# Score blocks of gated linear attention on 32-wide column tiles, in one stretch, and the head norm's sum as two rounded parts

## The chip, the cores and the metric

The kernel runs on one core of a Trainium2 chip. The metric is the time on the device in microseconds (us): the median of three runs, 2439.63 us, between 2439.05 and 2439.84. The engines are TensorE (PE in the rows; PEld is its loading of weights), VectorE (DVE), ScalarE (ACT), GpSimd (POOL) and SyncE (SP). Each runs its own instructions in order and waits for others on semaphores.

## The reference, cut to what matters

The model has two layers, an even one (retention and a gated linear recurrence) and an odd one (gated linear attention, GLA), each followed by an MLP. It handles 1024 prompt positions and 8 samples of 8 positions, so 1088 columns in all. The change lies in the odd layer. For each of 4 heads:

```python
def step(s, blk):                      # one chunk of the sequence
    qc, kc, vc, gc = blk
    b = jnp.cumsum(gc, axis=1)
    diff = b[:, :, None] - b[:, None, :]
    w = jnp.exp(jnp.where(causal, diff, -jnp.inf))
    scores = jnp.einsum('bihd,bjhd,bijhd->bhij', qc, kc, w)
    o = einsum(scores, vc) + einsum(qc * jnp.exp(b), s)
    s = s * jnp.exp(b_last)[..., None] + einsum(kc * jnp.exp(b_last - b), vc)
    return s, o
...
o = head_rms(o) * norm_w               # head_rms: x * rsqrt(mean(x*x) + EPS)
mix = (silu(r) * o) @ w_out
```

The weight `w` depends on row, column and channel at once, so the scores are not one plain product of q and k.

## The kernel before, in words

Activations lie with channels on the 128 partitions and positions along the columns. The 1088 columns are handled in groups of 384, 384 and 320. Each large projection multiplies two rounded parts: the high part of a weight tile (WH) by the high and the low part of the activation (RA or RB), and the low part of the weight (WL) by the high part; these are the many matmuls of L732, recorded in pairs WH, WH and single WL. In the records a tile of the rounded type is called f32 too.

In the odd layer a chunk is 128 positions (8 for each head, and a ninth of 64 sample positions). The order of all work there is one list, `odd_schedule` (L232), which every engine walks. For a chunk (h, c) it has these items:

- `S`: a group of a projection, cut in two halves of 12 matmuls of L732. They fill the time of TensorE between the items of the chunk.
- `A`: three transposes (L1211, L1213) of decayed keys and values, then the full 128x128 product of keys and queries (L1220), then the coarse levels of the score (L1153).
- `A2`: the fine levels (L1159). Between `A` and `A2` lies one half of an `S`.
- `B`: the output product and the update of the state, of the chunk one place earlier.
- `CO`, `CU`: the same for the samples of the ninth chunk, with very narrow matmuls.

The scores come from seven levels. At level v the chunk is cut in blocks of 2 x 2^v positions; the right half's queries meet the left half's keys, both scaled relative to the middle of the block (tile `gLV`, inside GA). The coarse levels v = 6, 5, 4 write their rectangle straight into the square of the score bank; the fine levels v = 3 to 0 each make a whole 128 x 64 product beside it, of which VectorE then copies only the blocks near the diagonal with a predicate (L2495, L2499). The levels are made by VectorE (L2450 differences, L2475 to L2479 products) with ScalarE's exponentials (L1750 to L1754) between; TensorE waits for each level with `lev_ready`. `gsc_done` tells VectorE that a chunk's scores are there, `gsc_masked` that a score bank is free again. Ordinary fp32 matmuls (all those on GA, SMALL and ONES) are recorded as two passes, each with its own weight load.

The head norm: `GN1` squares the two halves of a head's output (ScalarE, L1791) and adds them (VectorE, L2541); `GNM` multiplies the sum by a matrix of ones to add over partitions (L1300) and ScalarE takes its logarithm (L1798); `GN2` scales the output. This happens 11 times with a `GNM` of its own; the twelfth is L1307.

Of the kernel before, what the change touches and what calls it, by code (L numbers as in the profile page):

```python
# [35 lines left out]
SPLIT = 4  # L36
# [265 lines left out]
def build(nc, xT, ws, prm_in, csa, csg, cs_in, wla, wli, wg2_in, st_ret, st_lru, st_conv, st_gla,  # L302
          yT, retp_o, rets_o, lru_o, conv_o, glap_o, glas_o, x_spill):
    ctx = ExitStack()
    with ctx:  # L305
# [26 lines left out]
        ONES = sb("ONES", [P, P])  # L332
# [160 lines left out]
        gSQ = OD[:, 1792:2560]  # L493
        gSC = [MK[:, 0:CH], MK[:, CH:2 * CH]]
# [43 lines left out]
        def place(h, c):  # L538

            return PLACES.index((h, c))  # L540

# [188 lines left out]
        def _(pe):  # L730
# [61 lines left out]
            def rms_group(g, r):  # L792

                s, size = GROUPS[g]
                nc.tensor.matmul(PS[:, ms_bank(r, g), 0:size], ONES[:, :], RS[:, s:s + size],
                                 start=True, stop=True).then_inc(ms_done, 1)
# [158 lines left out]
            def last_rms(g):  # L955

                s, size = ENDS[g]
                pe.wait_ge(square_used, 7 * 4 + 7 * (g + 1) - g // 2)
                if g:
                    pe.wait_ge(rs_log, 3 * 4 + g)  # L960
                if g < 2:
                    nc.tensor.matmul(PS[:, 7, 0:size], ONES[:, :], RS[:, s:s + size],
                                     start=True, stop=True).then_inc(ms_done, 1)
                else:

                    nc.tensor.matmul(PS[:, 7, 0:size], ONES[:, :], RS[:, s:s + size], start=True, stop=False,
                                     skip_group_check=True)
                    pe.wait_ge(square_ready, 8 * 4 + KT * 3)
                    nc.tensor.matmul(PS[:, 7, 0:size], ONES[:, :], last_square(KT - 1, size), start=False, stop=True,
                                     skip_group_check=True).then_inc(ms_done, 1)  # L970


            def head_sum(item):

                g, h = item[1:]
                size = GROUPS[g][1]
                if h == 0:
                    pe.wait_ge(rn_sq, g + 1)

                    pe.wait_ge(kv_copied, 2 * before("RA", item))  # L980
                if h == 2:
                    pe.wait_ge(sc_masked, before("RA", item))
                if h == 3 and g < 2:
                    pe.wait_ge(s_updated, states_before(item))
                nc.tensor.matmul(PS[:, norm_bank(g, h), 0:size], ONES[:, :], NB[:, h, 0:size],
                                 start=True, stop=True).then_inc(rn_ms, 1)

            ident = CST[:, A_ID:A_ID + P]
            for item in even:
                kind = item[0]  # L990
                if kind in "GS":
                    u = item[1]
                    if u == 0:

                        pe.wait_ge(consts_set, 1)
                        for _ in range(16):
                            nc.tensor.matmul(PS[:, 7, 0:P], ONES[:, :], ONES[:, :], start=True, stop=True)
# [139 lines left out]
            def score(h, c, levels):  # L1137
# [5 lines left out]
                last = None  # L1143
                for v in reversed(levels):

                    pe.wait_ge(lev_ready, nth("Q", e, v))
                    both = gLV[e % 2][:, v, loc:loc + n]
                    if v >= FINE:

                        width = 1 << v  # L1150
                        for left in range(0, n, 2 * width):
                            right = slice(left + width, left + 2 * width)
                            last = nc.tensor.matmul(flat[left:left + width, right], both[:, left:left + width], both[:, right],  # L1153
                                                    start=True, stop=True)
                        continue
                    keys = both if v else gK(h)[:, s:s + n]
                    at = n + n // 2 * v
                    out = flat[0:n, at:at + n // 2].rearrange("p (b n) -> p b n", n=1 << v)
                    last = nc.tensor.matmul(out, keys, halves(both, v)[1], start=True, stop=True)  # L1159
                return last  # L1160

            ident = CST[:, G_ID:G_ID + P]
            for item in odd:
# [30 lines left out]
                elif kind == "A":  # L1194
# [21 lines left out]
                    if k > 1:  # L1216

                        pe.wait_ge(gsc_masked, k - 1)
                    flat = PS[:, score_bank(k), :]
                    nc.tensor.matmul(flat[0:n, 0:n], gK(h)[:, s:s + n], gQ(h)[:, s:s + n], start=True, stop=True)  # L1220
                    score(h, c, range(SPLIT, LEVELS) if c < LAST else ())
                elif kind == "A2":
                    h, c = item[1:]
                    score(h, c, range(SPLIT) if c < LAST else range(SLEVELS)).then_inc(gsc_done, 1)
# [68 lines left out]
                elif kind == "GNM":  # L1293
                    h, g = item[1:]
                    size = GROUPS[g][1]
                    if (h, g) != (GH - 1, 2):
# [3 lines left out]
                        nc.tensor.matmul(PS[:, 7, 0:size], ONES[:, :], gSQ[:, 0:size], start=True, stop=True).then_inc(gn_ms, 1)  # L1300

            def last_head_sum():
# [3 lines left out]
                for v in range(2):  # L1306
                    last = nc.tensor.matmul(PS[:, 7, 0:320], ONES[:, :], gSQ[:, 384 * v:384 * v + 320], start=v == 0, stop=v == 1)  # L1307
# [13 lines left out]
        def _(act):  # L1321
# [34 lines left out]
            def rstd(r):  # L1356
                other(ACT.Ln)
                act.wait_ge(consts_set, 2)
# [341 lines left out]
            for item in odd:  # L1700
# [36 lines left out]
                elif kind == "XE":  # L1737
# [6 lines left out]
                    if v == 0:  # L1744
                        s = GROUPS[g][0]
                        act.wait_ge(b_ready, softened(e))
                        if e > 1:

                            act.wait_ge(gsc_done, 3 * (e - 1))
# [59 lines left out]
                elif kind in ("MIX", "MH"):  # L1809
                    k = item[1]  # L1810
                    if k == 0:

                        act.wait_ge(gsc_done, len(PLACES))
# [31 lines left out]
        def _(dve):  # L1845
# [522 lines left out]
            for item in odd:  # L2368
# [34 lines left out]
                elif kind == "SPD":  # L2403
# [4 lines left out]
                    for c in range(3 * g0, 3 * g1):  # L2408
                        s, n = CHUNKS[c]
                        keep = ONES[:, 0:n] if c < LAST else CST[:, G_RS:G_RS + TS]  # L2410
# [29 lines left out]
                elif kind == "X":  # L2440
# [4 lines left out]
                    if e > 1:  # L2445

                        dve.wait_ge(gsc_done, 3 * (e - 1))
# [34 lines left out]
                elif kind == "A2":  # L2482
# [6 lines left out]
                    dve.wait_ge(gsc_done, k + 1)  # L2489
# [45 lines left out]
                elif kind == "GN1":  # L2535
# [5 lines left out]
                    V.tensor_tensor(gSQ[:, 0:size], gSQ[:, 0:size], gSQ[:, 384:384 + size], ALU.add).then_inc(gn_sum, 1)  # L2541
# [189 lines left out]
```

## Time and profile before

| | before |
|---|---|
| median of 3 runs | 2439.63 us |
| profiled execution, its own time | 2441.21 us |
| its span | 2439.1 us |
| PE busy | 2423.2 us (99%) |
| PE weight loads busy | 2380.3 us (98%) |
| DVE busy | 1305.2 us (54%) |
| POOL busy | 1211.9 us (50%) |
| ACT busy | 796.2 us (33%) |
| mean granted TensorE clock | 0.993 |

Busy is the time in which at least one instruction of the engine was under way. Matmuls are pipelined, so the duration of one (its latency) says little; what one costs is the distance from its start to the start of the next. The chunks of the odd layer lie between 1202 and 1592 us of the span. The granted clock is 1.00 at 2.4 GHz and 0.50 at 1.2 GHz; a mean between them says how much of a stretch ran at either.

### The profile page before, as it was taken

How to read it: one execution, taken by the hardware profiler on the slowest of the kernel's cores; microseconds unless marked ns; L12 is line 12 of the kernel's file. 1: busy time of each engine (PE TensorE's matmuls, PEld its weight loads, DVE VectorE, ACT ScalarE, POOL GpSimd, SP SyncE). 2: the span in 40 equal slices, each digit the busy share in tenths (PEclk: the TensorE clock that was granted, in tenths of full speed). 3: DMA queues.
4: the chain of work that ended last, by engine and by line, in shares of the span. 5: the costliest groups of instructions: out<-in, count | busy, mean ns of one | idle time of the engine just before them, and what ended most of it. 6: DMA issues, size and time to landing. Idle time of an engine off the chain costs nothing. (4 is left out here: it accounts for less than half of the span.)

```text
span 2439.1 us, 42031 instructions
## 1 busy us (share of the span) xinstructions
PE 2423.2 (99%) x16160; PEld 2380.3 (98%) x16160; DVE 1305.2 (54%) x2047; ACT 796.2 (33%) x1254; POOL 1211.9 (50%) x1445
## 2 busy tenths in 40 slices
PE   9999999999999999999999999999999999999998
PEld 9999999999999999999999999999999999999998
DVE  6763354345545545566666665554345545445566
ACT  4711442222222223223444564442222222222234
POOL 2454136465675666675201111146565665666681
PEclk9999999999999999999999999999999999999999
DMA  4123031111111111113111111131111111111112
GB/s 151 35 63 89 26 119 44 53 44 44 52 44 44 52 53 41 47 53 117 47 42 63 47 50 58 34 128 44 44 44 53 53 44 44 53 45 43 53 53 83
DMA packets 41023, 140.04 MB, mean 57 GB/s; under 512 B 6320, under 2 KB 10032, under 8 KB 39696
## 3 DMA queue, kind: packets, MB, share of 16 engines
q1 hardware_dynamic: 32768, 106.78, 13.8%
q10 hardware_dynamic: 8080, 30.78, 3.5%
q8 instruction: 128, 2.10, 0.4%
q14 instruction: 47, 0.39, 0.0%
HBM read 120.42 MB, written 14.88 MB: 55 GB/s over the span
## 5 line engine op out<-in xcount | busy, mean ns | idle before, releaser
L732 PE MATMUL PS<-RB,WH 128*128 128x384 f32 (+1 forms) x4368 | 1087.7, 330 | 0.0
L732 PEld LDWEIGHTS PS<-RB,WH 128*128 128x128 f32 x4368 | 773.5, 189 | 7.5 <-issue 3.6
L732 PE MATMUL PS<-RA,WH 128*128 128x272 f32 (+2 forms) x3520 | 769.0, 309 | 1.3 <-DVE RA L1868 0.7
L732 PE MATMUL PS<-RB,WL 128*128 128x384 f32 (+1 forms) x2232 | 731.6, 328 | 0.0
L638 POOL TENSOR_TENSOR WH<-WR,FEW 128x256 fp32r<-128x256 f32 x420 | 320.1, 792 | 622.3 <-PE PS L732 593.0
L732 PEld LDWEIGHTS PS<-RA,WH 128*128 128x128 f32 x3520 | 586.9, 188 | 5.8 <-DVE RA L1868 1.0
L732 PE MATMUL PS<-RA,WL 128*128 128x272 f32 (+2 forms) x1760 | 540.6, 307 | 0.0
L732 PEld LDWEIGHTS PS<-RB,WL 128*128 128x128 f32 x2232 | 421.4, 189 | 0.0
L642 POOL TENSOR_TENSOR WL<-WR,WH 128x256 fp32r<-128x256 f32 x420 | 372.8, 917 | 0.0
L732 PEld LDWEIGHTS PS<-RA,WL 128*128 128x128 f32 x1760 | 330.7, 188 | 0.0
L1967 DVE TENSOR_TENSOR X<-PS,X 128x544 f32<-128x544 f32 x280 | 202.6, 724 | 205.2 <-PE PS L732 205.1
L1908 DVE SCALAR_TENSOR_TENSOR RAW<-PS,RS 128x384 f32<-128x384 f32 (+1 forms) x192 | 97.0, 533 | 351.1 <-PE PS L732 317.9
L732 PE MATMUL PS<-RA,WS 128*128 128x272 f32 x2016 | 272.1, 288 | 0.0
L732 PEld LDWEIGHTS PS<-RA,WS 128*128 128x128 f32 x2016 | 260.5, 188 | 0.0
L661 POOL TENSOR_TENSOR WL<-WR,WH 128x512 fp32r<-128x512 f32 x168 | 155.2, 938 | 183.4 <-ACT WH L1400 183.4
L650 POOL TENSOR_TENSOR WL<-WR,WH 128x256 fp32r<-128x256 f32 x88 | 67.0, 792 | 336.5 <-ACT WH L1698 336.5
L1381 ACT ACTIVATE RAW<-RAW 128x384 f32<-128x384 f32 (+1 forms) x192 | 92.2, 505 | 332.2 <-DVE RAW L1908 332.2
L1919 DVE TENSOR_TENSOR RA<-RAW,RA 128x544 fp32r<-128x544 f32 (+1 forms) x112 | 142.9, 1294 | 26.3 <-ACT RA L1389 17.4
L661 POOL TENSOR_TENSOR WS<-WR,WS 128x256 fp32r<-128x256 f32 x112 | 119.1, 1064 | 14.6 <-ACT WS L1413 14.6
L1967 DVE TENSOR_TENSOR GA<-PS,GA 128x544 f32<-128x544 f32 x112 | 81.2, 725 | 80.0 <-PE PS L732 79.3
L1892 DVE TENSOR_TENSOR X<-PS,EB 128x384 f32<-128x384 f32 (+1 forms) x48 | 25.4, 535 | 116.6 <-PE PS L732 116.6
L1348 ACT ACTIVATE RB<-X,FEW 128x1088 fp32r<-128x1088 f32 x24 | 28.7, 1205 | 161.9 <-DVE X L1892 125.7
(237 smaller groups left out, 2370.8 us busy)
## 6 DMA issues: line engine op xcount, KB each, us to landing
WR<-ws SPq DMA_DIRECT2D x189, 512.0 KB, 3.5
EB<-xT ACTq DMA_DIRECT2D x8, 544.0 KB, 5.9
x_spill<-X ACTq DMA_DIRECT2D x8, 544.0 KB, 3.1
EB<-x_spill ACTq DMA_DIRECT2D x8, 544.0 KB, 6.8
GA<-st_gla ACTq DMA_DIRECT2D x4, 1024.0 KB, 4.8
glas_o<-GA ACTq DMA_DIRECT2D x4, 1024.0 KB, 4.6
yT<-X SPq DMA_DIRECT2D x16, 208.0 KB, 1.9
X<-xT ACTq DMA_DIRECT2D x4, 544.0 KB, 6.0
```

Of the source, the lines that this page charges most:

```text
L638: nc.gpsimd.tensor_tensor(WH[:, slot, QC * q:QC * (q + 1)], WR[:, slot, QC * q:QC * (q + 1)], ZERO[:, 0:1].to_broadcast([P, QC]), ALU.add) ...
L642: nc.gpsimd.tensor_tensor(WL[:, slot, QC * q:QC * (q + 1)], WR[:, slot, QC * q:QC * (q + 1)], WH[:, slot, QC * q:QC * (q + 1)].bitcast(F32 ...
L650: nc.gpsimd.tensor_tensor(WL[:, slot, QC * q:QC * (q + 1)], WR[:, slot, QC * q:QC * (q + 1)], WH[:, slot, QC * q:QC * (q + 1)].bitcast(F32 ...
L661: return nc.gpsimd.tensor_tensor(out, of, high.bitcast(F32), ALU.subtract)
L732: return nc.tensor.matmul(out, lhsT, rhs, start=start, stop=stop, skip_group_check=True)
L1348: A(dst[:, 0, k, :], X[:, k, :], ACT.Copy, scale=scale).then_inc(h_high, counts)
L1381: A(RAW[:, j, grp(g)], RAW[:, j, grp(g)], ACT.Square).then_inc(sq_done, 1)
L1892: V.tensor_tensor(X[:, m, s:s + size], PS[:, bank(n0 + m, g), 0:size], EB[:, at(m), s:s + size], ALU.add).then_inc(psum_free, 2)
L1908: V.scalar_tensor_tensor(RAW[:, j, s:s + size], PS[:, 3 * (j % 2) + g, 0:size], 0.0, RS[:, s:s + size], ALU.max, ALU.mult).then_inc(psum_f ...
L1919: return V.tensor_tensor(BS[:, slots, 1, q, :], of, BS[:, slots, 0, q, :].bitcast(F32), ALU.subtract)
L1967: last = V.tensor_tensor(pair_of(to), PS[:, bank0:bank0 + 2, 0:BN], pair_of(to), ALU.add)
```

## The change

1. The scores of a chunk are all computed in item `A2`, behind the half `S`; item `A` keeps only the transposes. The wait for a free score bank (`gsc_masked`) moves with them.
2. Each score matmul is cut in blocks of 32 rows of output (`BLOCK`), each of which uses 32 columns of weights. The 128x128 product of keys and queries becomes four products 32x32 on the diagonal; level 6 becomes two of 32x64; levels 5 and 4 stay as they are, on tiles of 32 and 16; each fine level becomes four products of 32x16.
3. `gsc_done` is raised by the matmul of level 0 of each block, so four times per chunk, and the waits on it count blocks (`scored`).
4. For the head norm VectorE now makes, after the sum, a rounded high part and the rest as a rounded low part (two more instructions), and `GNM` becomes two matmuls of the rounded type in place of one of fp32. For that the matrix ONES is of the rounded type, and made by a tensor_scalar at the start; other users read it as fp32 (`ONE`).

```diff
-        ONES = sb("ONES", [P, P])
+        ONES = sb("ONES", [P, P], F32R)
+        ONE = ONES[:, :].bitcast(F32)
...
+        gSQR = RAWR[:, :, :].rearrange("p k t -> p (k t)")[:, 1792:2560]
...
+        def scored(places):
+            return sum(CHUNKS[c][1] // BLOCK for _, c in PLACES[:places])
...
-            def score(h, c, levels):
+            def score(h, c):
...
-                for v in reversed(levels):
+                key, query = gK(h)[:, s:s + n], gQ(h)[:, s:s + n]
+                block = lambda b: slice(b, b + BLOCK)
+                for b in range(0, n, BLOCK):
+                    nc.tensor.matmul(flat[block(b), block(b)], key[:, block(b)], query[:, block(b)], start=True, stop=True)
+                for v in reversed(range(LEVELS if c < LAST else SLEVELS)):
                     pe.wait_ge(lev_ready, nth("Q", e, v))
                     both = gLV[e % 2][:, v, loc:loc + n]
+                    width = 1 << v
                     if v >= FINE:
-                        width = 1 << v
                         for left in range(0, n, 2 * width):
                             right = slice(left + width, left + 2 * width)
-                            last = nc.tensor.matmul(flat[left:left + width, right], both[:, left:left + width], both[:, right],
-                                                    start=True, stop=True)
+                            for b in range(left, left + width, BLOCK):
+                                rows = slice(b, b + min(width, BLOCK))
+                                nc.tensor.matmul(flat[rows, right], both[:, rows], both[:, right], start=True, stop=True)
                         continue
-                    keys = both if v else gK(h)[:, s:s + n]
                     at = n + n // 2 * v
-                    out = flat[0:n, at:at + n // 2].rearrange("p (b n) -> p b n", n=1 << v)
-                    last = nc.tensor.matmul(out, keys, halves(both, v)[1], start=True, stop=True)
-                return last
+                    for b in range(0, n, BLOCK):
+                        out = flat[block(b), at + b // 2:at + (b + BLOCK) // 2].rearrange("p (b n) -> p b n", n=width)
+                        last = nc.tensor.matmul(out, (both if v else key)[:, block(b)], halves(both[:, block(b)], v)[1],
+                                                start=True, stop=True)
+                        if v == 0:
+                            last.then_inc(gsc_done, 1)
...
-                    if k > 1:
-                        pe.wait_ge(gsc_masked, k - 1)
-                    flat = PS[:, score_bank(k), :]
-                    nc.tensor.matmul(flat[0:n, 0:n], gK(h)[:, s:s + n], gQ(h)[:, s:s + n], start=True, stop=True)
-                    score(h, c, range(SPLIT, LEVELS) if c < LAST else ())
                 elif kind == "A2":
                     h, c = item[1:]
-                    score(h, c, range(SPLIT) if c < LAST else range(SLEVELS)).then_inc(gsc_done, 1)
+                    if place(h, c) > 1:
+                        pe.wait_ge(gsc_masked, place(h, c) - 1)
+                    score(h, c)
...
-                        nc.tensor.matmul(PS[:, 7, 0:size], ONES[:, :], gSQ[:, 0:size], start=True, stop=True).then_inc(gn_ms, 1)
+                        mm(PS[:, 7, 0:size], ONES[:, :], gSQR[:, 384:384 + size], True, False)
+                        mm(PS[:, 7, 0:size], ONES[:, :], gSQR[:, 0:size], False, True).then_inc(gn_ms, 1)
...
-            V.memset(ONES[:, :], 1.0).then_inc(consts_set, 1)
+            link(V.memset(EPST[:, 1:2], 1.0))
+            V.tensor_scalar(ONES[:, :], EPST[:, 1:2].to_broadcast([P, P]), 0.0, None, ALU.add).then_inc(consts_set, 2)
             V.memset(EPST[:, 0:1], EPS).then_inc(consts_set, 1)
-            V.memset(EPST[:, 1:2], 1.0).then_inc(consts_set, 1)
...
-                    V.tensor_tensor(gSQ[:, 0:size], gSQ[:, 0:size], gSQ[:, 384:384 + size], ALU.add).then_inc(gn_sum, 1)
+                    first, second = gSQ[:, 0:size], gSQ[:, 384:384 + size]
+                    link(V.tensor_tensor(first, first, second, ALU.add))
+                    link(V.tensor_scalar(gSQR[:, 384:384 + size], first, 0.0, None, ALU.add))
+                    V.tensor_tensor(gSQR[:, 0:size], first, gSQR[:, 384:384 + size].bitcast(F32), ALU.subtract).then_inc(gn_sum, 1)
```

TensorE's rows of one full chunk, from the transposes to a few matmuls behind the fine levels, as they stand before (L732 on RB and WH or WL is the projection, GA holds keys, queries and levels; the sizes are those of the output):

```order
L1213 MATMUL PS<-CST,GA 128x128 x2
L1220 MATMUL PS<-GA 128x128
L1153 MATMUL PS<-GA 64x64
L1153 MATMUL PS<-GA 32x32 x2
L1153 MATMUL PS<-GA 16x16 x4
L732 MATMUL PS<-RB,WH 128x384 x2
...
L732 MATMUL PS<-RB,WL 128x384
L1159 MATMUL PS<-GA 128x64 x4
L732 MATMUL PS<-RB,WH 128x384 x2
```

And the same place of TensorE's program as it stands now (L738 is the old L732, L1226 the old L1213):

```order
L1226 MATMUL PS<-CST,GA 128x128 x2
L738 MATMUL PS<-RB,WH 128x384 x2
...
L738 MATMUL PS<-RB,WL 128x384
L1152 MATMUL PS<-GA 32x32 x4
L1164 MATMUL PS<-GA 32x64 x2
L1164 MATMUL PS<-GA 32x32 x2
L1164 MATMUL PS<-GA 16x16 x4
L1169 MATMUL PS<-GA 32x16 x16
L738 MATMUL PS<-RB,WH 128x384 x2
```

Twelve score matmuls in two places have become 28 in one, behind the half projection.

VectorE's rows around the first `GN1`, before (L2522 updates the state, L2450 makes level differences, L2541 adds the squares, L2495 begins the predicated copies of a chunk's scores):

```order
L2522 SCALAR_TENSOR_TENSOR SMALL<-SMALL,PS 128x256
L2450 TENSOR_TENSOR GA<-X 128x256
L2541 TENSOR_TENSOR SMALL<-SMALL 128x384
L2495 COPY_PREDICATED SMALL<-CST,PS 128x128
L2499 COPY_PREDICATED SMALL<-CST,PS 128x64
```

And now, with the old L2450 as L2461, L2541 as L2553 and L2495 as L2506:

```order
L2461 TENSOR_TENSOR GA<-X 128x256
L2553 TENSOR_TENSOR SMALL<-SMALL 128x384
L2554 TENSOR_SCALAR RAWR<-SMALL 128x384
L2555 TENSOR_TENSOR RAWR<-SMALL,RAWR 128x384
L2506 COPY_PREDICATED SMALL<-CST,PS 128x128
```

Two instructions stand between the sum and the next chunk's copies, 11 times in the program.

## Rows read from the trace of the kernel before

**Rows 1.** The page: the span, then each engine's busy time and share.

```profile
span 2439.1 us, 42031 instructions
PE 2423.2 (99%) x16160; PEld 2380.3 (98%) x16160; DVE 1305.2 (54%) x2047; ACT 796.2 (33%) x1254; POOL 1211.9 (50%) x1445
```

**Rows 2.** Windows of the odd layer's chunks: length, busy us of each engine, granted clock.

```profile
1255.00:1271.00 16.00, 16.00 (x93) 14.62 (x92) 6.73 (x18) 6.18 (x14) 2.77 (x4) 0.79 0.09 34
1350.00:1366.00 16.00, 16.00 (x104) 15.00 (x106) 10.04 (x23) 11.29 (x24) 3.12 (x4) 0.89 0.11 34
1450.00:1470.00 20.00, 20.00 (x119) 18.62 (x118) 10.68 (x25) 11.74 (x23) 3.13 (x4) 0.84 0.09 27
1580.00:1590.00 10.00, 10.00 (x69) 9.06 (x69) 3.16 (x8) 2.75 (x5) 2.56 (x4) 0.83 0.01 2
1200.00:1600.00 400.00, 398.37 (x2895) 377.47 (x2894) 245.59 (x659) 198.69 (x405) 65.56 (x88) 0.97 0.15 50
```

**Rows 3.** Timeline of TensorE, item A of a chunk: start us, length of the group.

```profile
1215.29 0.27 PE L1211 MATMUL PS<-CST,GA 128*128 128x128 f32 x1
1215.39 0.38 PE L1213 MATMUL PS<-CST,GA 128*128 128x128 f32 x2
1215.61 0.39 PE L1220 MATMUL PS<-GA 128*128 128x128 f32 x2
1215.93 0.55 PE L1153 MATMUL PS<-GA 128*64 128x64 f32 x14
1216.41 0.62 PE L732 MATMUL PS<-RB,WH 128*128 128x384 f32 x2
1216.87 0.35 PE L732 MATMUL PS<-RB,WL 128*128 128x384 f32 x1
1217.05 0.52 PE L732 MATMUL PS<-RB,WH 128*128 128x384 f32 x2
```

**Rows 4.** Timeline of TensorE, item A2 of the chunk before that one.

```profile
1211.43 1.00 PE L1159 MATMUL PS<-GA 128*128 128x64 f32 x8
1212.24 0.59 PE L732 MATMUL PS<-RB,WH 128*128 128x384 f32 x2
1212.67 0.33 PE L732 MATMUL PS<-RB,WL 128*128 128x384 f32 x1
1212.85 0.51 PE L732 MATMUL PS<-RB,WH 128*128 128x384 f32 x2
```

**Rows 5.** Window on L1153 alone: length, PE busy and matmuls under way, PEld busy.

```profile
1216.18:1216.30 0.12, 0.12 (x12) 0.11 (x12) 1.00 0.00 0
```

**Rows 6.** Timeline of TensorE around two GNM, of 384 and of 320 columns.

```profile
1237.52 0.81 PE L1300 MATMUL PS<-SMALL,ONES 128*128 128x384 f32 x2
1238.16 0.27 PE L1211 MATMUL PS<-CST,GA 128*128 128x128 f32 x1
...
1302.44 0.70 PE L1300 MATMUL PS<-SMALL,ONES 128*128 128x320 f32 x2
1302.98 0.27 PE L1211 MATMUL PS<-CST,GA 128*128 128x128 f32 x1
```

**Rows 7.** Timeline of VectorE at the first GN1.

```profile
1233.45 0.56 DVE L2541 TENSOR_TENSOR SMALL<-SMALL 128x384 f32<-128x384 f32 x1 [1.32 <-ACT SMALL L1791]
```

**Rows 8.** Line L1159: what its engine's idle time waited for (us, times).

```profile
  DVE GA L2479: 3.7, 7
  DVE GA L2475: 0.5, 2
```

**Rows 9.** Timelines of VectorE and TensorE around one such wait.

```profile
1506.46 0.56 DVE L1884 TENSOR_TENSOR SMALL<-PS,RS 128x384 f32<-128x384 f32 x1 [3.77 <-PE PS L732]
1521.21 0.88 DVE L2475 TENSOR_TENSOR GA<-GA 128x192 f32<-128x192 f32 x1
1522.14 0.43 PE L1159 MATMUL PS<-GA 128*128 128x64 f32 x2 [0.16 <-DVE GA L2475]
```

**Rows 10.** Timeline of TensorE at the start of the program.

```profile
1.07 6.15 PE L997 MATMUL PS<-ONES 128*128 128x128 f32 x32 [1.07 <-DVE FEW L2094]
7.66 0.59 PE L732 MATMUL PS<-RA,WH 128*128 128x384 f32 x2 [0.45 <-DVE RA L2107]
```

**Rows 11.** Timeline of TensorE in the first head's ninth chunk.

```profile
1256.91 4.05 PE L732 MATMUL PS<-SMALL,GA 128*128 128x8 f32 x24
```

More of the change, by code:

```diff
@@ L794, in rms_group @@
                 s, size = GROUPS[g]
-                nc.tensor.matmul(PS[:, ms_bank(r, g), 0:size], ONES[:, :], RS[:, s:s + size],
+                nc.tensor.matmul(PS[:, ms_bank(r, g), 0:size], ONE, RS[:, s:s + size],
                                  start=True, stop=True).then_inc(ms_done, 1)
@@ L961, in last_rms @@
                 if g < 2:
-                    nc.tensor.matmul(PS[:, 7, 0:size], ONES[:, :], RS[:, s:s + size],
+                    nc.tensor.matmul(PS[:, 7, 0:size], ONE, RS[:, s:s + size],
                                      start=True, stop=True).then_inc(ms_done, 1)
                 else:
-                    nc.tensor.matmul(PS[:, 7, 0:size], ONES[:, :], RS[:, s:s + size], start=True, stop=False,
+                    nc.tensor.matmul(PS[:, 7, 0:size], ONE, RS[:, s:s + size], start=True, stop=False,
                                      skip_group_check=True)
                     pe.wait_ge(square_ready, 8 * 4 + KT * 3)
-                    nc.tensor.matmul(PS[:, 7, 0:size], ONES[:, :], last_square(KT - 1, size), start=False, stop=True,
+                    nc.tensor.matmul(PS[:, 7, 0:size], ONE, last_square(KT - 1, size), start=False, stop=True,
                                      skip_group_check=True).then_inc(ms_done, 1)
@@ L984, in head_sum @@
                     pe.wait_ge(s_updated, states_before(item))
-                nc.tensor.matmul(PS[:, norm_bank(g, h), 0:size], ONES[:, :], NB[:, h, 0:size],
+                nc.tensor.matmul(PS[:, norm_bank(g, h), 0:size], ONE, NB[:, h, 0:size],
                                  start=True, stop=True).then_inc(rn_ms, 1)
@@ L996, in _ @@
                         for _ in range(16):
-                            nc.tensor.matmul(PS[:, 7, 0:P], ONES[:, :], ONES[:, :], start=True, stop=True)
+                            nc.tensor.matmul(PS[:, 7, 0:P], ONE, ONE, start=True, stop=True)
                         first_step(0, RA0, 0)
@@ L1306, in last_head_sum @@
                 for v in range(2):
-                    last = nc.tensor.matmul(PS[:, 7, 0:320], ONES[:, :], gSQ[:, 384 * v:384 * v + 320], start=v == 0, stop=v == 1)
+                    last = nc.tensor.matmul(PS[:, 7, 0:320], ONE, gSQ[:, 384 * v:384 * v + 320], start=v == 0, stop=v == 1)
                 last.then_inc(gn_ms, 1)
@@ L2409, in _ @@
                         s, n = CHUNKS[c]
-                        keep = ONES[:, 0:n] if c < LAST else CST[:, G_RS:G_RS + TS]
+                        keep = ONE[:, 0:n] if c < LAST else CST[:, G_RS:G_RS + TS]
                         if c == LAST:
```

13 lines of the change are left out of this document (6 added, 7 removed).

## The prediction

> **What bounds the kernel now.** I read the page first: TensorE is busy 2423.2 of 2439.1 us, VectorE 54%, ScalarE 33% [rows 1]. So the time is the sum of TensorE's distances from start to start, and an edit counts by what it does to that sum, unless it makes TensorE wait. The windows of the odd layer say the same for the 400 us in which the change lies: 398.37 us busy for TensorE, 245.59 for VectorE, 198.69 for ScalarE [rows 2]. Next I read the timelines of one chunk, which give starts. The reader should ignore the lengths there (0.27 us for one transpose is its latency; the next starts 0.11 later).
>
> **The scores, part by part.** There are 32 full chunks (4 heads of 8). In one of them, before:
> - KQ and the coarse levels run from 1215.61 to 1216.41, 0.80 us [rows 3]. The first three projection matmuls behind them take 1216.41 to 1217.05, 0.64, where three such matmuls otherwise take 0.52 (173 ns each: 1217.05 is followed by the same pattern all along, and in rows 4 the WL at 1212.67 starts 0.18 before the next). That is 0.12 lost at the change of kind.
> - The fine levels: 1211.43 to 1212.24, 0.81, and 0.61 in place of 0.52 behind them, 0.09 lost [rows 4].
> Together 1.82 us per chunk.
>
> After the change I count, in passes (two per fp32 matmul): 4 diagonal products 8, level 6 4, level 5 4, level 4 8, fine levels 32, so 56 passes in one block. I call T the time from the first of their starts to where the last is through with its tile. Around T stand: the transposes now run into the projection, 0.09, as L1159 did [rows 4]; going from 128-wide weights to narrow ones, 0.10 (the two KQ passes and the coarse block start 0.32 apart, where two passes of 128 cost 0.11 each, as the transposes do: 0.32 - 0.22) [rows 3]; coming back, 0.11, and 0.12 on the first projection matmuls as now [rows 3]. After = 0.42 + T, and the saving per chunk is 1.40 - T.
>
> What is T? The trace of before has no such block, so I bound it from both sides.
> - Low end: the tiles work side by side. In the window 1216.18 to 1216.30 twelve passes of 32 and 16 columns are under way within 0.12 us, 10 ns each [rows 5]; one pass of 32x32 alone cannot be that short, since a pass with 128 columns of weights costs 0.81/8 = 0.10 us [rows 4], so one of 32 about 0.025. Four column tiles each take a quarter of the passes; the fullest has 2 diagonal, 2 of level 6 (64 moving columns, double), 2 of level 5, 2 of level 4 and 8 fine ones, 16 passes or 18 counts of 0.028: T = 0.50, and 0.90 us saved per chunk, 29 us in all.
> - High end: 14 passes of L1153 take 1215.93 to 1216.41, 34 ns each [rows 3]. With 56 of them T = 1.90 and every chunk costs 0.50 more, +16 us.
> Between ends so far apart I go by the row that it is nearest to. The 34 ns hold two changes of tile width inside them, which the new block does not have, so the 10 ns of rows 5 are nearer; but those twelve passes are a short run that may have been waiting ready in TensorE's queue, while 56 passes and 56 weight loads have to be issued. I take 18 ns, T = 1.0, 0.40 saved per chunk: 32 x 0.40 = 12.8 us.
>
> Here the Trainium skill speaks against the change. "TensorE: Matmul & The Clock Gate", section "Back-to-back issue gap", gives small matmuls a floor of about 25 ns from start to start. By that figure the estimate would be 56 x 25 ns = 1.40 us, and the saving would be nil. The trace does not agree for a short run: twelve passes in 0.12 us [rows 5] are 10 ns each. No row of before shows a long one.
>
> The fourth kind, the ninth chunk of each head (4 in all, 16 passes in place of 8, the same two changes of width): I cost it at nothing, within 0.3 us each.
>
> **Waits in front of the scores.** The levels come from VectorE, and TensorE already waits for them: 3.7 us over 7 and 0.5 over 2 occasions, its weight loads and matmuls counted apart [rows 8]. One of them in detail: VectorE gets its input from TensorE at 1506.46, and from there its own chain with ScalarE runs 15.6 us to the end of level 0 at 1522.09, upon which TensorE starts at 1522.14 [rows 9]. What TensorE saves between those two moments it gives back as waiting. A group of three chunks lasts 400/12 = 33 us, so half of its saving (15.6 of 33) is lost where the levels are that late. Taking half of the 12 groups for it: 12.8 x 1/2 x 1/2 = 3.2 us lost. Queued behind the waiting matmul is all of TensorE's program, so such a wait counts in full. Moving KQ and the coarse levels behind the half projection softens this only by what little of them now stands before the late level; I give it nothing.
>
> The wait for a free score bank moves to a later place; it was not a wait before, and stays none.
>
> **The norm.** A GNM of fp32 costs 1238.16 - 1237.52 = 0.64 us at 384 columns and 0.54 at 320 [rows 6]. Two rounded matmuls cost 2 x 0.173 = 0.35 and 2 x 0.147 = 0.29. So 8 x 0.29 + 3 x 0.25 = 3.1 us less. VectorE does two instructions more, each about the 0.56 us of the sum [rows 7], 11 times, 12 us of an engine with over 150 us free in this stage [rows 2]. They end at about 1235.1 in place of 1234.0, and the GNM starts at 1237.52 [rows 6, 7]: hidden, by the projection half in between. Behind them on VectorE stands the copy of the next chunk's scores, which is needed only a chunk (about 10 us) later. If that cover were gone, it would cost up to 1.1 us x 11 = 12 us.
>
> **The start.** ONES is ready some 0.2 us later. TensorE's warm-up with it is followed by a wait of 0.45 us for VectorE's first operand [rows 10]: hidden.
>
> **The sum.** -12.8 + 3.2 - 3.1 = -12.7 us. The profiled execution's own time is 2441.21 us, 2.1 above its span, and the median shown is 2439.63, 1.6 below it; the saving carries over whole: 2439.6 - 12.7 = 2426.9, say 2427. What a measurement of this kernel can tell from no change is 0.2%, 4.9 us.
>
> **The rivals.**
> - *Full overlap.* The tiles bind and not the issue: T = 0.50. -29 us, of which the late levels keep more (a quarter, 7), and -3 for the norm: 2415. For it speak the twelve passes of rows 5; against it that nothing shows so dense a stream for longer. 0.13.
> - *The pace of issue eats it.* If the passes come no faster than one in 24 to 26 ns, T is 1.34 to 1.46 and the scores give 2 to -2 us; only the norm's 3 remain: 2435 to 2439. This is what the skill's floor in the same section would do (2436.5 by its 25 ns). Against it: rows 5. 0.15.
> - *The slower side: the narrow stream costs as in the block of now.* One mechanism, in the 32 blocks of A2: TensorE can't issue or load the narrow passes at under 34 ns, because each brings its own weight load and the wait on a level at its head. +16 - 3 = +13: 2453. It decides from a pace of about 26.7 ns on, where the scores lose what the norm gains. For it: the only long block in the trace has that pace [rows 3]. Against it: its inner changes of width. 0.10.
> - *VectorE's chain takes it.* If the levels are late in nearly all groups once TensorE is faster, half of everything is lost, and the two new instructions of GN1 push the chain a further 1.1 us in some: -12.8/2 - 3.1 + 4 = -5.5: 2434. For it: 9 waits are there already [rows 8]. Against: VectorE is idle 150 us of 400, much of it waiting for TensorE [rows 2, 9]. 0.10.
> - *The clock.* Around each head's ninth chunk the clock falls to 1.2 GHz (means 0.79, 0.89, 0.84, 0.83 over 16, 16, 20, 10 us: 3.4 + 1.8 + 3.2 + 1.7 = 10 us lost) [rows 2], from the matmuls with 8 moving columns on [rows 11]. If the narrow blocks make it fall once more per group, at the 1.7 us of the smallest of these, 12 x 1.7 = 20 us are lost: 2447. Against: the coarse block of 16 and 32 columns ran at 1.00 [rows 5]. One fall more or fewer at a head's end moves any case by 1.7. 0.06.
>
> My forecast has 0.46, with a range of its own of 2419 to 2435 (T from 0.78 to 1.22).
>
> **How the numbers follow.** Faster by more than 4.9 us: the forecast, full overlap, and most of the chain's case, 0.46 + 0.13 + 0.09, and a little of the pace's case, 0.03: 0.71. Same: 0.12 + 0.01 + 0.01 and a little: 0.14. Slower: 0.10 + 0.05: 0.15. The range reaches from 2413, beyond full overlap, to 2446: it leaves out the 34 ns case and the worst of the clock, and little below.
>
> **What would show each step.** In the timeline after, one block on GA between two projection matmuls; T is the distance from the first start on L1152 to the start of L738 behind L1169 less 0.11: 1.0 if I am right, 0.5 or 1.9 for the rivals. The sum over PE's score lines would fall. L1169's idle time on VectorE's products should grow from some 2 us of matmuls to about 5; the GNM's two matmuls should stand 0.35 us in all, with no wait for L2555. The windows of rows 2 should show the clock at 0.97 over the stage. I am wrong if T is over 1.2, if the waits for levels exceed 6 us, or if the granted clock falls in windows without narrow sample work.

## The result and the profile after

The changed kernel takes 2410.49 us in the median of 4 runs (2410.07 to 2411.48), the kernel before beside it 2439.34: a ratio of 0.9882, with a 95% interval of 0.9870 to 0.9894. That is 28.9 us less. The forecast was 2427 with a range from 2413 to 2446, so the direction was right, the size was not, and the time lies outside the range. The profiled execution of the kernel before took 2441.21 us, 1.9 above the median beside the changed kernel, that of the changed kernel 2410.41, at its median: the two profiles differ by more than the medians do.

The page of the changed kernel, to be read against [rows 1]: TensorE still bounds it, with 33 us less busy.

```profile
span 2408.5 us, 44166 instructions
PE 2390.0 (99%) x17216; PEld 2348.4 (98%) x17216; DVE 1317.0 (55%) x2069; ACT 796.1 (33%) x1254; POOL 1221.6 (51%) x1445
```

TensorE's timeline of one chunk, the same place as [rows 3] and [rows 4] (start us, length of the group):

```profile
1207.95 0.27 PE L1224 MATMUL PS<-CST,GA 128*128 128x128 f32 x1
1208.06 0.38 PE L1226 MATMUL PS<-CST,GA 128*128 128x128 f32 x2
1208.20 0.60 PE L738 MATMUL PS<-RB,WH 128*128 128x384 f32 x2
1208.63 0.35 PE L738 MATMUL PS<-RB,WL 128*128 128x384 f32 x1
1208.82 0.52 PE L738 MATMUL PS<-RB,WH 128*128 128x384 f32 x2
...
1210.22 0.34 PE L738 MATMUL PS<-RB,WL 128*128 128x384 f32 x1
1210.48 0.27 PE L1152 MATMUL PS<-GA 128*32 128x32 f32 x8
1210.57 0.35 PE L1164 MATMUL PS<-GA 128*32 128x64 f32 x15
1210.75 0.21 PE L1169 MATMUL PS<-GA 128*32 128x16 f32 x3
1210.77 0.18 PE L1164 MATMUL PS<-GA 128*16 128x16 f32 x1
1210.80 0.45 PE L1169 MATMUL PS<-GA 128*32 128x16 f32 x29
1211.18 0.62 PE L738 MATMUL PS<-RB,WH 128*128 128x384 f32 x2
1211.63 0.34 PE L738 MATMUL PS<-RB,WL 128*128 128x384 f32 x1
1211.81 0.51 PE L738 MATMUL PS<-RB,WH 128*128 128x384 f32 x2
```

All 56 passes of a chunk start between 1210.48 and 1211.18, where the projection goes on: 0.70 us in place of 0.80 + 0.81, and T, without the 0.11 of the return, is 0.59. Note also that passes of L1169 start at 1210.75, ahead of one of L1164 at 1210.77, though it stands before them in the program: column tiles work each for itself.

The norm's first sum, as in [rows 6]:

```profile
1235.14 0.34 PE L738 MATMUL PS<-RB,WL 128*128 128x384 f32 x1
1235.56 0.59 PE L738 MATMUL PS<-RAWR,ONES 128*128 128x384 f32 x2
1235.99 0.27 PE L1224 MATMUL PS<-CST,GA 128*128 128x128 f32 x1
```

This one takes 0.43 us from start to start; 7 of the 8 of 384 columns take 0.35 to 0.36 in place of 0.64, and the 3 of 320 take 0.30 in place of 0.54. VectorE's side of it, as in [rows 7]:

```profile
1232.07 0.56 DVE L2553 TENSOR_TENSOR SMALL<-SMALL 128x384 f32<-128x384 f32 x1 [1.32 <-ACT SMALL L1802]
1232.67 0.36 DVE L2554 TENSOR_SCALAR RAWR<-SMALL 128x384 fp32r<-128x384 f32 x1
1233.06 0.56 DVE L2555 TENSOR_TENSOR RAWR<-SMALL,RAWR 128x384 fp32r<-128x384 f32 x1
1233.54 0.30 DVE L2506 COPY_PREDICATED SMALL<-CST,PS 128x128 f32<-128x128 uint32 x1
...
1234.94 0.47 DVE L2533 SCALAR_TENSOR_TENSOR SMALL<-SMALL,PS 128x256 f32<-128x256 f32 x1
```

The two parts are ready at 1233.6, 1.9 us before the sum. But the sum also waits for the update of the state (L2533), which stands behind them on VectorE and ends at 1235.4. It starts 0.42 us behind the projection's last matmul; the other ten start 0.15 to 0.18 behind theirs, and so does the first one in the run with the scores alone, where VectorE's two instructions are missing and the update ends at 1234.2. The two instructions thus cost about 0.25 us here, and nothing that shows at the other ten places.

TensorE's waits in the odd layer (us in total, times, longest), and two blocks in which they fall, in the timeline:

```profile
PE PS L1169 <- DVE GA L2490: 3.4, 8, 0.8
```

```profile
1223.46 0.24 PE L1169 MATMUL PS<-GA 128*32 128x16 f32 x6
1224.37 0.26 PE L1169 MATMUL PS<-GA 128*32 128x16 f32 x8 [0.67 <-DVE GA L2490]
1224.91 0.53 PE L1169 MATMUL PS<-GA 128*32 128x16 f32 x16 [0.28 <-DVE GA L2490]
...
1423.81 0.26 PE L1152 MATMUL PS<-GA 128*32 128x32 f32 x4
1424.87 0.24 PE L1169 MATMUL PS<-GA 128*32 128x16 f32 x4 [0.81 <-DVE GA L2490]
1425.35 0.47 PE L1169 MATMUL PS<-GA 128*32 128x16 f32 x8 [0.23 <-DVE GA L2490]
```

TensorE waits in front of level 2 and again in front of level 1. I measured each of the 36 blocks from its first start to the start behind it. Without a wait a full one lasts 0.70 and one of a ninth chunk 0.36; what goes beyond adds up to 6.5 us (0.35 of it, at 1251, is a wait for ScalarE behind the block). The same count before (0.81 and 0.46 for item A2) gives 3.2 us.

The stretches of the stage in which the clock stood at 1.2 GHz: the sum over five windows of before, then over four of after.

```profile
1466.84:1470.25 3.41, 3.41 (x12) 3.41 (x12) 0.76 (x2) 0.00 (x0) 0.00 (x0) 0.50 0.00 0
...
sum 20.46, PE 20.46 PEld 18.32 DVE 8.51 ACT 5.45 POOL 6.84; mean PE 4.09 PEld 3.66 DVE 1.70 ACT 1.09 POOL 1.37
```

```profile
1437.01:1443.83 6.82, 6.82 (x25) 6.09 (x22) 6.72 (x14) 4.89 (x10) 3.75 (x4) 0.50 0.00 0
...
sum 17.03, PE 17.03 PEld 15.65 DVE 12.77 ACT 6.91 POOL 5.81; mean PE 4.26 PEld 3.91 DVE 3.19 ACT 1.73 POOL 1.45
```

Half of that time is lost: 10.2 us before, 8.5 after. This holds for these two executions, not for the kernels. Other executions of the kernel before took from 2434.28 us, at a mean granted clock of 0.996, to 2441.33, at 0.994, so the same program loses some us more or less to the clock; the profiled one is among the slower. The account of the two profiled spans:

| | us |
|---|---|
| 32 blocks, 1.61 to 0.70 | -29.1 |
| 4 blocks of a ninth chunk, 0.26 + 0.46 to 0.36 | -1.4 |
| changes of kind around them, 0.21 before; 0.09 in, 0.11 out and 0.01 behind the transposes after | 0 |
| longer waits for levels, 3.2 to 6.5 | +3.3 |
| the norm's sums, 8 x 0.29 + 3 x 0.24 | -3.0 |
| 3.4 us less at 1.2 GHz | -1.7 |
| new waits of the projection (L738) for VectorE, outside the blocks | +0.6 |
| sum | -31.3 |
| difference of the spans, 2408.5 - 2439.1 | -30.6 |

The other 0.7 us I have not traced.

### The profile page after: what moved, and what is told of

It is laid out like the page before. It is cut to its first block and busy times, and to the rows that moved or that the text cites. A ratio compares the mean times of both kernels' runs of the same rounds, so it can differ in the third digit from the quotient of the medians.

```text
span 2408.5 us, 44166 instructions
## 1 busy us (share of the span) xinstructions
PE 2390.0 (99%) x17216; PEld 2348.4 (98%) x17216; DVE 1317.0 (55%) x2069; ACT 796.1 (33%) x1254; POOL 1221.6 (51%) x1445
## 5 line engine op out<-in xcount | busy, mean ns | idle before, releaser
L738 PE MATMUL PS<-RB,WH 128*128 128x384 f32 (+1 forms) x4368 | 1086.7, 330 | 0.0
L738 PEld LDWEIGHTS PS<-RB,WH 128*128 128x128 f32 x4368 | 773.2, 189 | 6.4 <-issue 3.3
L738 PE MATMUL PS<-RA,WH 128*128 128x272 f32 (+2 forms) x3520 | 769.1, 309 | 1.6 <-DVE RA L1879 0.7
L738 PE MATMUL PS<-RB,WL 128*128 128x384 f32 (+1 forms) x2232 | 731.4, 328 | 0.0
L738 PEld LDWEIGHTS PS<-RA,WH 128*128 128x128 f32 x3520 | 586.9, 188 | 6.1 <-DVE RA L1879 1.0
L738 PE MATMUL PS<-RA,WL 128*128 128x272 f32 (+2 forms) x1760 | 540.6, 307 | 0.0
L738 PEld LDWEIGHTS PS<-RB,WL 128*128 128x128 f32 x2232 | 421.3, 189 | 0.0
L738 PEld LDWEIGHTS PS<-RA,WL 128*128 128x128 f32 x1760 | 330.7, 188 | 0.0
L738 PE MATMUL PS<-RA,WS 128*128 128x272 f32 x2016 | 272.1, 288 | 0.0
L738 PEld LDWEIGHTS PS<-RA,WS 128*128 128x128 f32 x2016 | 260.5, 188 | 0.0
L1359 ACT ACTIVATE RB<-X,FEW 128x1088 fp32r<-128x1088 f32 x24 | 28.7, 1206 | 160.7 <-DVE X L1903 125.3
```

Source lines behind the costliest of these rows:

```text
L738: return nc.tensor.matmul(out, lhsT, rhs, start=start, stop=stop, skip_group_check=True)
L1359: A(dst[:, 0, k, :], X[:, k, :], ACT.Copy, scale=scale).then_inc(h_high, counts)
```

## The experiments

The theory at the outset (A): the gain comes from column tiles working side by side. Rivals: it comes from having the scores in one stretch (B), or mostly from the norm (C). All times are medians. Each kernel was run beside the kernel before, which took 2439.59 us beside the first four, 2440.80 beside the four from "Blocks of 64" to "Less copying", and 2439.51 beside the last three. A distance from the changed kernel is thus uncertain by some 1.5 us for the middle four.

**The norm alone.** The norm's edit put into the kernel before, whose scores keep their order and widths.

```diff
-                        nc.tensor.matmul(PS[:, 7, 0:size], ONES[:, :], gSQ[:, 0:size], start=True, stop=True).then_inc(gn_ms, 1)
+                        mm(PS[:, 7, 0:size], ONES[:, :], gSQR[:, 384:384 + size], True, False)
+                        mm(PS[:, 7, 0:size], ONES[:, :], gSQR[:, 0:size], False, True).then_inc(gn_ms, 1)
```

> The kernel before with the norm's part of the change alone (two rounded parts, two rounded matmuls, ONES of the rounded type). Theory A (the gain of 29 us comes from 32-column tiles working side by side): the norm gives 8 x 0.29 + 3 x 0.25 = 3.1 us, so about 2436. Rival B (the gain comes from having the scores in one stretch): the same 3.1 us. Rival C (the norm's part is worth far more than its matmuls, since ScalarE waits 23 us for them): 8 us or more, 2431 or less.

Measured: 2434.83 us, ratio 0.9979 (0.9970 to 0.9988), 4.8 us less; the interval, from 2.9 to 7.3 us, holds the 3.1 too. The two profiled spans are 5.7 apart. TensorE's sums give 3.0 of it, as expected; the stage has 17.1 us at 1.2 GHz where the profile of before has 20.5, which is 1.7; and the score blocks take 56.7 us in all in place of 57.7. C falls.

**The scores alone.** The changed kernel with the norm as before.

```diff
-                        mm(PS[:, 7, 0:size], ONES[:, :], gSQR[:, 384:384 + size], True, False)
-                        mm(PS[:, 7, 0:size], ONES[:, :], gSQR[:, 0:size], False, True).then_inc(gn_ms, 1)
+                        nc.tensor.matmul(PS[:, 7, 0:size], ONE, gSQ[:, 0:size], start=True, stop=True).then_inc(gn_ms, 1)
...
-                    link(V.tensor_scalar(gSQR[:, 384:384 + size], first, 0.0, None, ALU.add))
-                    V.tensor_tensor(gSQR[:, 0:size], first, gSQR[:, 384:384 + size].bitcast(F32), ALU.subtract).then_inc(gn_sum, 1)
```

> The changed kernel with the norm as before (one fp32 matmul, one sum on VectorE). Theory A and rival B: about 3 us above the changed kernel, 2413.5; the two parts add up. Rival C: 2418 or more. If the two VectorE instructions of the norm lengthen the waits for levels, they are gone here, and it is nearer to 2412.

Measured: 2414.91, ratio 0.9904 (0.9889 to 0.9919), 4.4 above the changed kernel, with 20.5 us at 1.2 GHz in the stage (1.7 lost against the changed kernel). Its waits on L1169 are 3.4 us as in the changed kernel, so VectorE's two instructions of the norm don't lengthen them. The parts add up within the noise: 24.7 + 4.8 = 29.5, against 28.9 for the whole change.

**One stretch without tiles.**

```diff
-BLOCK = 32
+BLOCK = 128
```

> The changed kernel with blocks of 128 columns: all scores in one stretch behind the half projection, but one 128x128 product of keys and queries, level 6 on 64 columns, and fine levels of 128x64, as before. Theory A: almost all of the scores' gain goes; the stretch takes 1.6 us per chunk, one return to the projection is spared and one change of width is added, so 2433 to 2437. Rival B: most of the gain stays, 2420 or less.

Measured: 2435.24, ratio 0.9983 (0.9974 to 0.9992), the time of the norm alone. The stretch in its timeline:

```profile
1210.24 0.38 PE L1153 MATMUL PS<-GA 128*128 128x128 f32 x2
1210.55 0.55 PE L1165 MATMUL PS<-GA 128*64 128x64 f32 x14
1211.03 1.11 PE L1170 MATMUL PS<-GA 128*128 128x64 f32 x8
1211.95 0.60 PE L738 MATMUL PS<-RB,WH 128*128 128x384 f32 x2
```

1.71 us, 0.10 more than the two parts of before, against one return spared. The one stretch is worth nothing by itself, against the kernel with the norm alone; B falls.

**Tiles in the old places.**

```diff
+                    score(h, c, True)     # item A: diagonal and coarse levels
...
+                    score(h, c, False)    # item A2: fine levels
```

> The changed kernel with 32-column tiles, but the diagonal and coarse levels in item A right behind the transposes and only the fine levels in A2, as they were placed before. Theory A: the passes are as fast, and only a second entry and return per chunk come on top (0.09 + 0.11 + 0.11 less what the transposes' return costs now): 0.2 to 0.3 us x 32 = 6 to 10 us above the changed kernel, 2417 to 2421. Rival B: the gain of the scores is gone, 2430 or more.

Measured: 2415.81, ratio 0.9907 (0.9892 to 0.9922), 5.3 above the changed kernel. Its blocks are 0.39 and 0.38 us. The profiled execution was its fastest, 2413.79 us, at a mean granted clock of 0.997 where the other three have 0.994, and so it can be compared with the profile of the changed kernel alone. Its span is 3.4 us longer, with 10.2 us at 1.2 GHz in the stage against 17.0, which gives 3.4 back; without that it would be 6.8 longer, in the range expected. With tiles, then, the one stretch is worth about 0.2 us per chunk.

**Blocks of 64.** The same with `BLOCK = 64`.

> The changed kernel with blocks of 64 columns: 2 diagonal products of 64x64, level 6 as one of 64x64, fine levels as two of 64x32; levels 5 and 4 stay on 32 and 16. Theory A1 (what sets a tile's pace is its load of weights, 27 ns for 32 columns, and tiles run side by side): two tiles side by side, each pass 53 ns, fine levels 8 passes per tile = 0.43, diagonal and level 6 together 4 x 53 = 0.21, two changes of width: block about 0.95 us, time 0.25 x 32 = 8 us above the changed kernel, 2418. Rival A2 (the pace is one pass issued every 10 ns, whatever the width): 34 passes take 0.35 us and the block gets shorter than 0.70: 2407 or less.

Measured: 2423.05, ratio 0.9928 (0.9912 to 0.9945), 12.6 above the changed kernel.

```profile
1210.47 0.34 PE L1153 MATMUL PS<-GA 128*64 128x64 f32 x4
1210.64 0.51 PE L1165 MATMUL PS<-GA 128*64 128x64 f32 x14
1211.08 0.66 PE L1170 MATMUL PS<-GA 128*64 128x32 f32 x16
1211.66 0.62 PE L738 MATMUL PS<-RB,WH 128*128 128x384 f32 x2
```

The block lasts 1.19 us, more than the 0.95 of A1 and far from the 0.7 or less of A2: fewer passes, and yet slower. The rival that issue sets the pace falls. The 16 fine passes take 0.58 with the return, 0.47 without: 8 on each of two tiles, 59 ns apart, where I had taken 53; the two changes of width cost most of the rest.

**Block by block.** The same 56 passes, the fine ones in another order. TensorE now waits for level 0, the last one made, in front of all of them.

```diff
-                        continue
-                    at = n + n // 2 * v
-                    for b in range(0, n, BLOCK):
+                fine = list(reversed(range(FINE if c < LAST else SLEVELS)))
+                pe.wait_ge(lev_ready, nth("Q", e, 0))
+                for b in range(0, n, BLOCK):
+                    for v in fine:
```

> The changed kernel with the fine levels issued block by block (all four levels of the first 32 columns, then of the next), same passes. Theory A1 with a look-ahead of few instructions (16 weight loads ahead at most, as counted from the start of sequencer instructions in the trace of before): eight passes in a row go to one tile, at most two tiles are busy at once, the 32 fine passes take 32 x 27 / 2 = 0.43 us or more in place of 0.35, up to 0.87 with no overlap; time 3 to 16 us above. Rival A2 (issue sets the pace): no change beyond the wait for level 0 standing earlier, within 1 us.

Measured: 2420.07, ratio 0.9919 (0.9903 to 0.9936), 9.6 above the changed kernel.

```profile
1211.04 0.27 PE L1152 MATMUL PS<-GA 128*32 128x32 f32 x8
1211.13 0.38 PE L1164 MATMUL PS<-GA 128*32 128x64 f32 x16
1211.36 0.86 PE L1173 MATMUL PS<-GA 128*32 128x16 f32 x32
1212.15 0.62 PE L738 MATMUL PS<-RB,WH 128*128 128x384 f32 x2
```

The fine part takes 0.79 us to the return, 0.68 without it, in place of about 0.30, with not one pass more. In the trace the passes of one tile start 31 to 32 ns apart, so 32 of them in 0.68 us mean that 1.5 tiles are at work on average. No wait stands in this block. This is the sharpest evidence for A: the gain hangs on neighbours in the program going to different tiles.

**Fine products twice.**

```diff
+                        for _ in range(2):
                             last = nc.tensor.matmul(out, (both if v else key)[:, block(b)], ...
```

> The changed kernel with each fine product computed twice into the same place: 88 passes per chunk in place of 56. What a fine pass costs when a stream is long: if 10 to 11 ns (as in the block of 0.70 us for 56), the block is 1.04 us. If the first passes were only fast because they were ready in TensorE's queue, the added ones come at 20 to 34 ns each, and the block is 1.3 to 1.8 us.

Measured: 2417.02 in one run. The block:

```profile
1210.42 0.27 PE L1152 MATMUL PS<-GA 128*32 128x32 f32 x8
1210.50 0.38 PE L1164 MATMUL PS<-GA 128*32 128x64 f32 x16
1210.73 0.81 PE L1170 MATMUL PS<-GA 128*32 128x16 f32 x64
1211.47 0.62 PE L738 MATMUL PS<-RB,WH 128*128 128x384 f32 x2
```

1.05 us with 88 passes against 0.70 with 56: 11 ns for each added pass. The pace holds in a long stream, and the doubt about the queue is settled. The time is only 6.5 us above the changed kernel, though 32 x 0.35 + 4 x 0.21 (the ninth chunks) = 12.0 us of passes came on top. The late levels give back 2.4 (what the blocks last beyond their length without a wait is 4.1 us in place of 6.5), and the clock 1.7 (13.7 us at 1.2 GHz); some 1.4 I have not traced.

**Less copying.** Levels 1 to 3 aren't copied into the scores, so the outputs lack their part.

```diff
+                    levels = 1
                     for v in range(levels):
```

> The changed kernel without the predicated copies of levels 1 to 3 of each chunk (left out of the scores), 2 to 3 VectorE instructions less per chunk, about 0.8 us. Theory D (the waits at the head of a group come from VectorE's own chain, which includes these copies): the blocks of scores that now last over 0.70 us (or 0.36 in the ninth chunk) get shorter, about 6.4 us of waiting become 2 to 4, time 2 to 4 us below the changed kernel. Rival E (the chain is set by ScalarE and by when TensorE's projections land): the waits stay, within 1 us.

Measured: 2406.95, ratio 0.9866 (0.9849 to 0.9882), 3.5 less than the changed kernel. But 1.7 of it is the clock of the profiled execution (13.7 us at 1.2 GHz), and the waits are hardly fewer:

```profile
PE PS L1169 <- DVE GA L2490: 2.9, 7, 0.9
```

The block at 1223 falls from 2.20 to 1.28 us, that of the first ninth chunk from 0.60 to 0.36, and the one at 1251 from 1.05 to 0.70. But the two latest, of ninth chunks again, go from 1.54 and 1.95 to 1.64 and 2.03, and the last ninth chunk's from 0.36 to 0.67. All 36 take 29.2 us in place of 30.3. Theory D holds for some early blocks and falls for the sum: 5.4 us of waiting are left, where it said 2 to 4, and rival E, which said a change within 1 us, is nearer.

**Scores a whole group later.**

```diff
-                s += (take(1) if p == 8 else []) + [("A",) + PLACES[k + 1]] + take(1)
+                s += (take(1) if p == 8 else []) + [("A",) + PLACES[k + 1]] + take(2 if p in (2, 5) else 1)
```

> The changed kernel with item A2 put behind a whole projection group, in place of half of one, at places 2 and 5 of each head (the first chunks of a group, where TensorE waits for levels): 2 us more for the levels. If the waits (1.5 us at 1223, 1.2 at 1332, 1.6 at 1424, 0.2 at 1497) are set by when the levels' chain starts, and not by TensorE's own progress, they go: 4 us less, 2406. Rival: VectorE, which walks the same list, does its copy out of the projection first, the levels come later by as much, and nothing changes.

Measured: 2409.97, ratio 0.9881 (0.9866 to 0.9896), no change that can be told from the changed kernel. The waits did move: the ninth chunks' blocks are all 0.36 us now, and the 36 blocks sum to 26.9 us in place of 30.3, so 3.1 us of waiting are left of 6.5. But other waits came (us in total, times, longest):

```profile
PE PS L738 <- ACT X L1790: 1.7, 3, 0.9
PE PS L1169 <- DVE GA L2490: 0.8, 2, 0.5
PE PS L738 <- DVE SMALL L2533: 0.8, 1, 0.8
```

and in the profiled execution the clock stood at 1.2 GHz for 20.5 us in place of 17.0, 1.7 lost. Both the theory and the rival missed: half of the wait for levels went, and what was gained turned into waits for ScalarE and VectorE and into clock.

**The samples on tiles.** The products of the ninth chunk with the sample states, 8 moving columns each.

```diff
-                            last = mm(PS[:, 6, 128 * v + LS * b:128 * v + LS * (b + 1)],
-                                      gSB[:, b, 128 * v:128 * (v + 1)], gQD[e % 2][:, loc:loc + LS],
-                                      False, v == 1 and b == NS - 1)
+                            whole = (b, v) == (NS - 1, 1)
+                            for at in range(0, 128, 128 if whole else BLOCK):
+                                end = at + (128 if whole else BLOCK)
+                                last = mm(PS[at:end, 6, 128 * v + LS * b:128 * v + LS * (b + 1)],
+                                          gSB[:, b, 128 * v + at:128 * v + end], gQD[e % 2][:, loc:loc + LS],
+                                          False, whole)
```

> The changed kernel with the sample products of item CO (16 per head, 128 columns of weights and 8 moving, 32 passes of 0.112 us = 3.6 us per head) cut into four column tiles of 32 each, all but the last product, which stays whole and so ends behind the others. Theory A: 120 passes at 11 ns = 1.3 us, 0.22 for the whole one, and 0.4 for two entries and returns: 1.7 us less per head, 6.7 us in all. Theory F (the clock falls because of these narrow products): the clock, which was at 1.2 GHz for 17.1 us of this stage in the changed kernel, stays at 2.4 more of the time, which gives up to 8.5 us on top; 2395 to 2404. Rival: the clock is unchanged, since narrower tiles keep TensorE no busier, 2404. Against both: the passes of 8 moving columns can't come faster than one weight load per tile of 28 ns allows, which four tiles still turn into 7 ns each.

Measured: 2396.95, ratio 0.9827 (0.9814 to 0.9841), 13.5 less than the changed kernel. Its timeline and the window of the whole stage, which answer to [rows 11] and the last of [rows 2]:

```profile
1254.39 0.72 PE L738 MATMUL PS<-SMALL,GA 128*32 128x8 f32 x64
```

```profile
1200.00:1600.00 400.00, 394.89 (x4583) 374.34 (x4582) 278.10 (x712) 213.47 (x423) 91.90 (x114) 1.00 0.19 67
```

The clock doesn't fall at all in the stage of this execution, which gives 8.5 us; the other 5 come from the passes. All five executions have a mean granted clock of 0.997 or 0.998 over the program, all four of the changed kernel 0.994, so the gain in clock is the kernel's and not this execution's. Theory F holds, and its rival falls.

**Both.** The sample tiles and the later scores in one kernel, a version that beats both.

> Both of the edits of e9_samples_tiled and e10_later_scores in one kernel, as the version that may beat the changed one: their gains add up, 2391 to 2400; less if the shorter sample stretch makes the levels of the next head late.

Measured: 2394.19, ratio 0.9822 (0.9808 to 0.9836), 16.3 less than the changed kernel and 45 less than the kernel before. The 2.8 against the sample tiles alone lie within the intervals. In its trace the clock does fall once in the stage, for 3.4 us from 1254.7 on, 2 us after the first tiled sample products started, and one of its five executions took 2399.85 us at 0.995: the tiles make such falls fewer, they don't rule them out.

## Why the prediction was wrong

- *What bounds the kernel* was right: TensorE's busy time fell by 33 us, its distances from start to start, waits and clock account for 31.3, and the span fell by 30.6.
- *T = 1.0, at 18 ns a pass* was the step that failed. T is 0.59, 10.5 ns a pass, and this alone is 0.41 x 32 = 13 us of the 16.4 that are missing. The bound from below, 0.50 from weight loads on four tiles side by side, was close: its form was right, with 31 to 32 ns a pass on one tile in place of 28 (which itself was above the 25 that I had just worked out). And [rows 5] had shown the pace. I misread that row a little: of its 12 passes under way, two are those of level 6, started before the window; the other ten start within 0.09 us, which is the same 10 ns each. I set the lower bound aside because the twelve passes might have been waiting in the queue. The doubled fine products show 11 ns in a stream of 88, and the order block by block shows what sets the pace: 31 to 32 ns on one tile, divided by the tiles at work.
- *The changes of kind.* I gave 0.42 us around T. It is 0.32: 0.09 going in, the return of 0.11, 0.11 on the projection's first matmuls, and 0.01 behind the transposes, in place of 0.09. There the projection's first matmuls take 0.09 more, but it starts behind the last transpose 0.08 sooner than another transpose would. That is 3 us in all.
- *The ninth chunks* I put at nothing, within 0.3 us each. They gave 0.36 each, 1.4 us in all.
- *The late levels*: +3.2 forecast, +3.3 measured, and this agreement is luck. I took a quarter of what TensorE saves, and it saved 29 us and not 12.8; the same quarter would have been 7. They wait, as I said, but mostly in four blocks of 36 (1202, 1223, 1332 and 1424, the last two of ninth chunks). Leaving three of a chunk's five copies out of VectorE's work more than halves the wait at 1223 and shortens none of the other three; what sets those stays open.
- *The norm*: -3.1 forecast, -3.0 in the trace. Its own run shows 4.8, with 1.7 of clock in the profiled execution. The two VectorE instructions are hidden in ten places of eleven; in the first they delay the update of the state, for which the sum waits too, by about 0.25 us. I had looked only at what the sum itself needs.
- *The clock* was a rival on the slow side only. Between the two profiled executions it helped: 3.4 us less at 1.2 GHz, 1.7 us. Between the medians nothing shows that it did: the profiled execution of before lies 1.9 us above its median, and 30.6 - 1.9 leaves 28.7, about the 28.9 measured.
- *The rivals.* Full overlap was the case that came true, with T = 0.59 against its 0.50. Its 2415 still missed the 2410.5, as it took 7 us for the late levels and the full 0.42. Of the issue floor of 25 ns, which the Trainium skill gives in "TensorE: Matmul & The Clock Gate", section "Back-to-back issue gap", the runs now say that it doesn't hold across column tiles: 11 ns for each added pass.
- *The start* cost nothing that shows: the first score passes start at 1202.17 before and at 1202.16 after.

## What to carry to other kernels

Where TensorE is full and narrow fp32 products stand in its stream, cut them to 32 columns of weights and put neighbours on different column tiles; the order decides as much as the width. Price such a block as passes per tile times the time of one on its tile, and believe a short dense run in the trace before a long average that has changes of width in it. Look at the granted clock too: here, thin products cost more by what they did to it (8.5 us) than tiles could save on their own length (5 us).

## What was not expected of the hardware

- Passes on different column tiles start out of program order (L1169 at 1210.75, L1164 at 1210.77), although I had written at the outset that each engine runs its instructions in order. One signal on the last product may then come too early; the kernel raises one for each tile. In "TensorE: Matmul & The Clock Gate", section "Part 3: Packing small matmuls — row/col tiling", the Trainium skill says that matmuls start and end strictly in order; this trace does not agree for the starts, and the ends in it are modelled. Whether a single signal would be safe wasn't tried.
- The sample products on tiles (64 passes of 8 moving columns in 0.72 us, where 16 passes of 128 columns of weights took 16 x 0.112 = 1.8) kept the clock at 2.4 GHz through 400 us in which it had stood at 1.2 for 17 to 20. In the kernel with both edits it stood there for 3.4.
- In traces of kernels that differ little the time at 1.2 GHz in the stage is 20.5, 17.0, 13.7 or 10.2 us, so 2 to 5 us of a small difference can be clock. It differs between executions of one kernel too (2434.28 us at a mean of 0.996 and 2441.33 at 0.994 for the kernel before), so it has to be read from the very execution that is compared.
